# Where a matmul's input starts: slice 0 of each input moved from 192 to 0 modulo 256 bytes

## The reference

```python
n1 = _rmsnorm(h, norm1_g[l])
xr, gr, cq, ckv, kr, g_rnn, g_att = jnp.split(n1 @ w_in[l], IN_SPLITS, axis=-1)
hr = _rg_lru(_causal_conv(xr, ...), rg_wa[l], rg_ba[l], rg_wx[l], rg_bx[l], rg_lambda[l])
...
h = h + mixed @ w_out[l]
h = h + _peer(_rmsnorm(h, norm2_g[l]), peer_wq[l], ..., peer_u[l], peer_v[l])
...
def swiglu_ffn(h, w_gate_up, w_down):
    gate, up = jnp.split(h @ w_gate_up, 2, axis=-1)
    return (jax.nn.silu(gate) * up) @ w_down
```

## Time and profile before

| | |
|---|---|
| median of 3 runs | 2131.07 us (2127.33 to 2135.39) |
| the profiled execution | 2142.68 us, of which the span from first to last instruction is 2140.9 |
| TensorE busy with matmuls | 2095.9 us, 17394 instructions |
| TensorE busy with weight loads | 2051.9 us |
| VectorE, ScalarE busy | 1421.1 us, 1153.3 us |
| mean granted clock of TensorE | 0.991 |

### The profile page before, as it was taken

One profiled execution on the slowest core, in us unless ns is written; L12 is line 12 of the kernel. 1 busy time (PEld: TensorE's weight loads), 2 busy tenths in 40 slices (PEclk: granted clock), 3 DMA queues, 4 the chain that ended last, 5 costly groups with the idle time before them and its releaser, 6 DMA issues.

```text
span 2140.9 us, 41500 instructions
## 1 busy us (share of the span) xinstructions
PE 2095.9 (98%) x17394; PEld 2051.9 (96%) x17394; DVE 1421.1 (66%) x2427; ACT 1153.3 (54%) x1950; POOL 451.2 (21%) x393
## 2 busy tenths in 40 slices
PE   8989999999999999999999999999999999989998
PEld 8988899999999999999999999899999999989998
DVE  6885466999877875555567655757656664747654
ACT  5764355544777765454556545445545544545443
POOL 2251120113888830000002002311002001112001
PEclk9999999999999999999999999989999999999999
DMA  6433244454444345555556454324554555433553
GB/s 235 170 126 116 99 169 170 169 186 165 151 145 151 139 166 191 196 197 193 187 192 230 167 197 165 131 99 169 188 196 173 183 189 186 159 117 141 195 197 118
DMA packets 53017, 359.34 MB, mean 168 GB/s; under 512 B 5920, under 2 KB 8512, under 8 KB 10208
## 3 DMA queue, kind: packets, MB, share of 16 engines
q1 hardware_dynamic: 52400, 356.04, 46.4%
q10 hardware_dynamic: 432, 0.64, 0.1%
HBM read 355.61 MB, written 1.05 MB: 167 GB/s over the span
## 4 chain that ended last, share of the span: by engine, by line
PE 90%; DVE 7%; ACT 2%; issue 1%; DMA 0%; POOL 0%; SPq 0%; ACTq 0%; DVEq 0%; POOLq 0%
PE ps L570 90%; DVE wlo L1223 3%; DVE oh L1481 1%; ACT whi L1882 1%; DVE csel L1485 1%; DMA raw<-in_w_dram 0%; DVE XC L1294 0%; DVE thT L1353 0%; DVE thT L1349 0%; DVE cT L1291 0%; PE ps L739 0%; DVE hT L1667 0%; DVE cT L1289 0%; ACT L2086 0%; ACT sqT L1963 0%
## 5 line engine op out<-in xcount | busy, mean ns | idle before, releaser
L1223 DVE TENSOR_TENSOR wlo<-raw,whi 128x1024 fp32r<-128x1024 f32 x667 | 866.6, 1299 | 526.3 <-ACT whi L1882 524.1
L1882 ACT ACTIVATE whi<-raw 128x1024 fp32r<-128x1024 f32 x667 | 707.7, 1061 | 708.9 <-PE ps L570 706.6
L570 PE MATMUL ps<-XB,whi 128*128 128x256 f32 x5280 | 927.3, 280 | 5.5 <-DVE wlo L1223 3.2
L570 PEld LDWEIGHTS ps<-XB,whi 128*128 128x128 f32 x5280 | 799.7, 188 | 8.3 <-ACT coefA L2060 3.0
L570 PE MATMUL ps<-XB,wlo 128*128 128x256 f32 x2640 | 733.3, 278 | 0.0
L570 PE MATMUL ps<-XA,whi 128*128 128x256 f32 (+1 forms) x2992 | 533.5, 282 | 6.4 <-DVE wlo L1223 6.2
L570 PEld LDWEIGHTS ps<-XB,wlo 128*128 128x128 f32 x2640 | 498.1, 189 | 0.0
L570 PEld LDWEIGHTS ps<-XA,whi 128*128 128x128 f32 x2992 | 458.1, 189 | 12.0 <-issue 9.7
L570 PE MATMUL ps<-XA,wlo 128*128 128x256 f32 (+1 forms) x1496 | 418.2, 280 | 0.0
L570 PEld LDWEIGHTS ps<-XA,wlo 128*128 128x128 f32 x1496 | 284.4, 190 | 0.0
L2354 POOL TENSOR_TENSOR accA<-accA,sq 128x256 f32<-128x256 f32 x37 | 36.1, 977 | 1016.2 <-ACT sq L2150 664.4
(11 more groups left out here) (383 smaller groups left out, 2233.1 us busy)
## 6 DMA issues: line engine op xcount, KB each, us to landing
raw<-in_w_dram SPq DMA_DIRECT2D x332, 1024.0 KB, 4.8
raw<-in_w_dram SPq DMA_DIRECT2D x4, 512.0 KB, 7.3
xin<-in_xin_dram SPq DMA_DIRECT2D x4, 272.0 KB, 6.5
hT<-in_xin_dram SPq DMA_DIRECT2D x1, 1024.0 KB, 11.6
binb<-in_binb_dram SPq DMA_DIRECT2D x1, 1024.0 KB, 8.3
Fraw<-in_cst_dram SPq DMA_DIRECT2D x2, 384.0 KB, 4.9
out_dram<-hT ACTq DMA_DIRECT2D x2, 256.0 KB, 2.4
out_dram<-hT SPq DMA_DIRECT2D x1, 256.0 KB, 2.3
```

What stands on the lines that cost most here:

```text
L570: return e.matmul(out, lhsT, rhs, start=start, stop=True, skip_group_check=True)
L1223: e.tensor_tensor(w_lo(u), w_raw(u), f32(w_hi(u)), ALU.subtract).then_inc(*sig("lo", u))
L1882: e.activation(w_hi(u), w_raw(u), AF.Copy).then_inc(*sig("hi", u))
```

## The change

It moves tensors by 64 bytes and narrows the gap behind slice 0 from 128 bytes to 64, so that slice 0 of each input starts at 0 modulo 256 bytes and the others stay where they were modulo 256. The skips behind take the 64 bytes back. No instruction is added, removed or put elsewhere in the order of any engine.

```diff
     def at(self, k, n=256):
-        o = self.step * k + (32 if k else 0) + self.tokens
+        o = self.step * k + (16 if k else 0) + self.tokens
         return slice(o - n, o)
...
-        sb(ctx, "skip0", [128, 16])
+        sb(ctx, "skip0", [128, 32])
         XB = Input(sb(ctx, "XB", [128, 2, 2112], F32R))
-        sb(ctx, "skip1", [128, 112])
+        sb(ctx, "skip1", [128, 96])
...
-        sb(pq, "skip2", [128, 32])
+        sb(pq, "skip2", [128, 48])
         XQ = Input(sb(pq, "XQ", [128, 2, 2112], F32R))
         pq.close()
-        sb(p1, "skip3", [128, 16])
+        sb(p1, "skip3", [128, 32])
         XA1 = Input(sb(p1, "XA1", [128, 2, 2624], F32R), 272, 320)
...
-        sb(p1, "skip4", [128, 48])
+        sb(p1, "skip4", [128, 32])
...
-        sb(p1, "skip5", [128, 16])
+        sb(p1, "skip5", [128, 32])
         OA = Input(sb(p1, "OA", [128, 2, 2112], F32R))
...
-        sb(p3, "skip6", [128, 32])
+        sb(p3, "skip6", [128, 48])
         XA = Input(sb(p3, "XA3", [128, 2, 2112], F32R))
...
-        sb(p3, "skip7", [128, 48])
+        sb(p3, "skip7", [128, 32])
...
-        sb(p3, "skip9", [128, 32])
+        sb(p3, "skip9", [128, 48])
         hid = ExitStack()
         hid_ = Input(sb(hid, "hid", [128, 2, 256 * NF + 64], F32R))
...
-        sb(cs, "skip10", [128, 32])
+        sb(cs, "skip10", [128, 16])
```

## The result

| | before | after |
|---|---|---|
| median, first comparison (4 runs each) | 2130.13 us (2127.33 to 2135.39) | 2149.53 us (2148.61 to 2151.64) |
| ratio, 95% interval | | 1.009 [1.0068, 1.0111] |
| median, second comparison (17 and 6 runs) | 2133.94 us (2126.26 to 2142.72) | 2148.35 us (2144.89 to 2152.44) |
| ratio, 95% interval | | 1.0065 [1.0039, 1.0092] |
| the profiled execution | 2142.68 us | 2151.64 us |

By the medians of the two comparisons the change costs 14 to 19 us. The page after shows the same kernel: the same instructions, TensorE busy for 98% of a span 8.9 us longer, 89% of the last chain at the same line, and the same wait for `wlo`.

The account below looks back on a forecast made before the run. TensorE's matmuls, their number times their pace, were taken to bound the kernel. All terms summed to 0 us against the profiled 2142.68, carried over to the median of the other executions, 2131.07: forecast 2131 us, range 2116 to 2144.

Parts of the forecast that it names:

- The step that failed: Whole kernel, 13,461 matmuls at 64: slice 0 at 0 was taken to leave their pace as 192 does, 0 us.
- the 272-column rows: `wa`/`wx` products on XC: 126.7 ns at starts 0 and 192, 123.3 at 64, so 0 was priced like 192.
- The term of the spread: Stretches anywhere in the kernel coming out at the other pace by chance, since later starts depend on waits: 4 us either way.
- The own price of slice 0: 1665 matmuls on slice 0 moving from 192 to 0: 118 ns as before, 0 us, between 6.3 less and 7.5 more.
- The rival of fast into slow: V stage, gate and up products: slice 0 throws fast stretches slow, 23 us, 2154; v stage alone 11 us, 2142; chance 0.12.
- With 192 the fast pace survives slice 0: Argument against the fast-into-slow case: in all three long fast stretches the fast pace outlasted slice 0 at 192.
- The rival of slow into fast: Slow stretches: slice 0 at 0 lifts them into the fast pace, 12 us, up to 18, so 2113 to 2123; chance 0.14.

Follow-up runs that it names:

- TensorE alone: Kernel with only matmuls of the same form, rest of the computation left out; slices at 0, 128 and 192 took 118.8, 120.0 and 117.8 ns, at 64 113.3 or 117.8.

## Why the prediction was wrong

**The step that failed** is "I take it that a slice 0 with the cost of 192 hands the pace on as 192 does: 0". The cost of 192 it nearly has (118.8 ns against 117.8), and it doesn't hand the pace on. Behind a run of 24 at 0 a fast stretch turned slow in the v stage (54 matmuls fewer in 349 us), in `hid` (18 or 19 fewer in each of f=0, f=1 and f=3) and with TensorE alone; a slow one turned fast in the v stage, in `hid` and with TensorE alone. The comparison itself was too simple as well: 192 kept the fast pace in every pass of the v stage, but with TensorE alone it lifted the slow one behind 9 of 19 slow entries. Price and hand-over are two properties of a start, and the 272-column rows could show the first alone.

**The term of the spread**, 4 us either way for stretches that come out at the other pace by chance, treated as chance what the change steers. The median moved by 14 to 19 us, beyond the range's upper end.

**The own price of slice 0**, taken as 0 between -6.3 and +7.5 us: the v stage's slice-0 units went from 2.83 to 2.85 us. 1 ns on 1665 matmuls would be 1.7 us. The term was small, as predicted, and was off by that.

**The rival of fast into slow** named the right mechanism and the right sign with a chance of 0.12. It had all or none of a stretch change over. In fact the v stage changed by half (3012 matmuls in the window, where 3066 was all fast and some 2960 all slow), which is 6.4 us instead of 11. The gate and up products changed by 0.03 us a block, and the down products, which it didn't name, gave 2.2 us in each of f=0, f=1 and f=3. That 2149.5 lies between its 2142 and its 2154 is partly luck. (Its 2500 matmuls at 64 in the v stage are low as well: seven eighths of 3066 are 2683, 12 us.) "With 192 the fast pace survives slice 0" was good evidence for 192 and none for 0.

**The rival of slow into fast** held as well, for blocks of 3: 2.83 to 2.77 us. By the four inputs that are mostly read in blocks the change costs nothing (ratio 0.9983). It was too weak to balance the runs of 24.

**What was right**: TensorE's pace is all that counts, waits for `wlo` stayed (9.8 and 10.2 us), VectorE's writes of XB in the v stage still take 415 to 421 ns, and no instruction moved. Of the Trainium skill's rule in "SBUF — State Buffer", Specifications, that reads go by lines of 16 bytes: four starts on such lines gave 113.3, 117.8, 118.8 and 120.0 ns here, so no run shows that rule as the one that decides.

## What to carry to other kernels

Where one instruction has two paces, compare layouts by how they leave the engine for the thousands of instructions behind the changed ones, and not by the price of the changed ones: the dearest slice here (128, 120.0 ns) made the fastest kernel, and the cheapest (64) a slower and more scattered one than before. Count matmuls in windows, before and after, for stretches that were fast and for those that were slow. A kernel of bare matmuls, with the start, the length of the run and several entries, answers in one run what a price taken from neighbouring rows can't. It must then be read in the whole kernel too: with TensorE alone 128 always left the fast pace, and behind the `oneB` groups it didn't.

## What the runs showed of the hardware

A 256-column matmul of this form, without any wait and at a granted clock of 1.00, takes 113.3 or 117.8 ns at the same addresses; the entry decides, and the pace then holds for hundreds of matmuls. The pace goes by both operands: with the stationary tile at 192 instead of 128, inputs at 0, 64, 128, 192 took 117.8, 120.0, 113.3 (or 117.8) and 120.0 ns. The fast pace was seen only where the input starts 64 bytes below the stationary tile modulo 256; twelve of the sixteen pairs of starts had other distances, three of them with eight entries and nine with two. A run of 24 at a start of 0 swapped the pace in the v stage and in `hid`, and with TensorE alone runs of 3, 6, 12 and 48 left the fast one. What inside the engine or SBUF has such a cycle no run here shows.
